# A hybrid trunk's first layer: convolution, time steps and head norms moved into the input projection

## The reference

```python
mods = silu(cvec) @ w_ada[l] + b_ada[l]            # shifts, scales, gates: sh1 sc1 g1 sh2 sc2 g2
h = rms(x, norm_w[l, 0]) * (1 + sc1) + sh1
u = h @ w_in                                       # 2832 columns: z, xbc, dt | q, k, v
xbc = silu(dwconv(xbc, conv_w, conv_b))            # 3 taps along the tokens, 768 channels -> xs, B, C
dt = softplus(dt_raw + dt_bias); g = dt * -exp(a_log)
y = bidirectional chunked scan(C, B, xs * dt, g)   # 8 heads of 64, both directions
y = rms((y + d_skip * xs) * silu(z), ssd_norm_w)
q, k = rms(q, q_norm), rms(k, k_norm)              # per head of 64
o = attention: context over context; each latent grid row over 8 rows + 128 cached keys
x = x + g1 * (concat(y, o) @ w_out)
h = rms(x, norm_w[l, 1]) * (1 + sc2) + sh2         # then the convolutional FFN
```

## Time and profile before

| | us |
|---|---|
| median of 3 runs | 3716.46 (3715.77 to 3718.22) |
| the profiled execution | 3712.03 |
| its span | 3710.4 |
| PE busy in the span | 3248.3 (88%) |
| DVE, ACT, POOL busy | 1863.4, 1364.7, 563.4 |
| mean granted TensorE clock | 0.936 of 2.4 GHz |

### The profile page before, as it was taken

How to read it: one execution, slowest core, us unless ns; L and a number is a source line. 1 busy time by engine, 2 the same in 40 slices (tenths; PEclk the granted TensorE clock), 3 DMA queues, 4 the chain that set the end, 5 groups by cost and what they waited for, 6 DMA issues and landing times. The chain is left out here.

```text
span 3710.4 us, 56967 instructions
## 1 busy us (share of the span) xinstructions
PE 3248.3 (88%) x22776; PEld 2966.8 (80%) x22776; DVE 1863.4 (50%) x3088; ACT 1364.7 (37%) x2312; POOL 563.4 (15%) x462
## 2 busy tenths in 40 slices
PE   5999386688939999999949999899978499999998
PEld 2999153466929999999929999677768499999998
DVE  4000366444277777753343300577753777777433
ACT  4111212676053333332233711455541433333322
POOL 1001064000033322200010001111100323221000
PEclk7999697899969999999979999899979699999999
DMA  6221501200021222164463521322122122222553
GB/s 279 84 92 46 215 4 72 104 2 24 23 92 67 82 72 72 49 214 145 131 244 109 167 90 47 138 89 86 66 101 75 36 72 84 77 72 71 201 170 130
DMA packets 133840, 370.12 MB, mean 100 GB/s; under 512 B 15232, under 2 KB 66816, under 8 KB 124496
## 3 DMA queue, kind: packets, MB, share of 16 engines
q1 hardware_dynamic: 124528, 335.82, 25.6%
q0 software_dynamic: 9056, 30.75, 2.3%
HBM read 282.56 MB, written 83.96 MB: 99 GB/s over the span
## 5 line engine op out<-in xcount | busy, mean ns | idle before, releaser
L83 PE MATMUL ffn__pair<-hf__acts,ffn__w_hi 128*128 128x288 f32 x2464 | 726.5, 295 | 115.0 <-DVE ffn__w_lo L807 115.0
L85 PE MATMUL ffn__pair<-hf__acts,ffn__w_hi 128*128 128x288 f32 x2464 | 728.5, 296 | 0.0
L84 PE MATMUL ffn__pair<-hf__acts,ffn__w_lo 128*128 128x288 f32 x2464 | 727.0, 295 | 0.0
L83 PEld LDWEIGHTS ffn__pair<-hf__acts,ffn__w_hi 128*128 128x128 f32 x2464 | 463.7, 188 | 116.3 <-DVE ffn__w_lo L807 116.3
L84 PEld LDWEIGHTS ffn__pair<-hf__acts,ffn__w_lo 128*128 128x128 f32 x2464 | 463.7, 188 | 0.0
L85 PEld LDWEIGHTS ffn__pair<-hf__acts,ffn__w_hi 128*128 128x128 f32 x2464 | 463.7, 188 | 0.0
L83 PE MATMUL ffn__pair<-hf__acts 128*128 128x384 f32 x1056 | 354.7, 336 | 8.5 <-DVE hf__acts L854 8.5
L85 PE MATMUL ffn__pair<-hf__acts 128*128 128x384 f32 x1056 | 354.4, 336 | 0.0
L84 PE MATMUL ffn__pair<-hf__acts 128*128 128x384 f32 x1056 | 354.4, 336 | 0.0
L83 PE MATMUL in__bank<-hm__h_lo,in__wt_hi 128*128 128x384 f32 x816 | 277.0, 340 | 10.3 <-DVE in__wt_lo L2053 5.3
L840 DVE SCALAR_TENSOR_TENSOR all__x_t<-all__x_t 128x127 f32<-128x127 f32 x352 | 271.2, 812 | 29.3 <-ACT all__x_t L709 29.2
(11 more groups left out here) (359 smaller groups left out, 6384.8 us busy)
## 6 DMA issues: line engine op xcount, KB each, us to landing
hf__raw<-w_down SPq DMA_DIRECT2D x100, 512.0 KB, 3.6
ffn_g<-all__x_t SPq DMA_DIRECT2D x44, 576.0 KB, 3.2
ffn__raw_odd<-ffn_g SPq DMA_DIRECT2D x132, 192.0 KB, 3.6
hf__raw<-w_up SPq DMA_DIRECT2D x44, 512.0 KB, 4.4
hm__raw<-w_t SPq DMA_DIRECT2D x34, 512.0 KB, 3.8
n0a__ada_w<-w_ada SPq DMA_DIRECT2D x16, 1024.0 KB, 10.3
n1a__ada_w<-w_ada SPq DMA_DIRECT2D x16, 1024.0 KB, 8.5
u_t<-in__out_t POOLq DMA_DIRECT2D x26, 576.0 KB, 3.1
```

The lines of the kernel that those rows point to most:

```text
L83: pe.matmul(out, w_hi, v_lo, start=first, stop=False)
L84: pe.matmul(out, w_lo, v_hi, start=False, stop=False)
L85: return pe.matmul(out, w_hi, v_hi, start=False, stop=last)
```

## The change

- The projection's tile order is now convolution, time steps, q, k; its loops are written out; the ring has four weight slots. While PE works on tile t, DVE, ACT and a few PE groups ("jobs", placed behind a bank of the next tile) process tile t-1: taps, SiLU and transposes; or squares, head sums, Ln, Exp and scaling. q and k go to `u0_t` already normed; convolution results stay in SBUF (`held`, and x_t's memory as `room`). The small chain of the time steps runs on DVE in the token half.
- Modulation groups 1 and 2 run in the token half of the projection, one step behind every second token block; the first norm keeps group 0, with 3 slots. Group 3 stays in the scan, with 2 slots in place of 4.
- The separate mask load, `conv_rows` and the head-norm block are gone, with their loads from device memory.
- Attention's keys, biases and values are loaded in the scan (`NaInputs.ahead`); q is loaded in the attention block, straight into `q_two`. Attention goes pair by pair.
- `y_tok` lies in x_t's memory; `out_project` loads x again from the input after the transposes.

```diff
-            ada = Modulation(s, d, mods, gains, ident, groups, 4, ps[NB:])
+            ada = Modulation(s, d, mods, gains, ident, groups, 3 if own_mods else 4, ps[NB:])
...
+def in_jobs():
+    jobs, after = [], {}
+    def put(t, b, job):
+        after.setdefault((t, b), []).append(len(jobs))
+        jobs.append(job)
+    for t in range(1, IN_TILES + 1):
+        prev = t - 1
+        if prev == DT_TILE:
+            put(t, 0, ("dt", 0, 0, 0))
+        elif prev < CONV - 1:
+            put(t, 1, ("conv", prev, 0, 4))
+            put(t, 1, ("conv", prev, 4, 4))
+            put(t, 2, ("conv", prev, 8, 1))
+        elif prev >= QK_FROM:
+            for b in range(NB):
+                put(t, b // 2, ("qk", prev - QK_FROM, b, 0))
+    return jobs, after
...
+                load(2)
+                load(3)
+                sp.dma_start(cw[:, :, :], d["ssd_conv"]).then_inc(small_in, 16)
+                sp.dma_start(half[:, :], d["half"]).then_inc(small_in, 16)
+                sp.dma_start(gain[:, :], d["qk_gain"]).then_inc(small_in, 16)
+                sp.dma_start(row[:, :], d["ssd_row"]).then_inc(row_in, 16)
+                sp.dma_start(tri[:, :, :], d["tri"]).then_inc(masks_in, 16)
+                ada.load_small(sp)
+                for n in range(ada.slots):
+                    ada.load(sp, n)
+                for t in range(4, IN_TILES):
+                    load(t)
...
+                ada.silu(act)
+                act.wait_ge(small_in, 48)
+                split_hi(0)
+                split_hi(1)
+                for t in range(IN_TILES):
                     for b in range(NB):
+                        evict(t, b)
+                        if b == 0 and 1 <= t <= CONV:
+                            silu(t - 1)
+                        for u in after.get((t, b), ()):
+                            read(u)
+                    split_hi(t + 2)
...
+                for t in range(IN_TILES):
+                    if t > QK_FROM:
+                        normalise(t - 1 - QK_FROM)
+                    if t < CONV:
+                        conv(t)
+                    elif t >= QK_FROM:
+                        square(t - QK_FROM)
+                    split_lo(t + 2)
+                normalise(IN_TILES - 1 - QK_FROM)
+                steps()
...
+                        if n % 2 and n // 2 < ada_steps:
+                            if n == 1:
+                                pe.wait_ge(t_out, NB * IN_TILES)
+                            if n // 2 == KT:
+                                ada.turn(pe, 0)
+                            ada.multiply(pe, n // 2)
...
-        ada = Modulation(s, d, mods, gains, ident, (3,), 4, ps[3:5])
+        ada = Modulation(s, d, mods, gains, ident, (3,), 2, ps[3:5])
...
-                sp.dma_start(dt[:, :, :, :].rearrange("p t w h -> p (t w h)"), d["u0_small"]).then_inc(dt_in, 16)
-                sp.dma_start(row[:, :], d["ssd_row"]).then_inc(row_in, 16)
                 sp.dma_start(state[:, 2:4, :], d["ssd_state"]).then_inc(state_in, 16)
                 sp.dma_start(z[:, :, :], d["u0_tok"][:, :, 0:SSD_W].rearrange("t p n -> p t n")).then_inc(z_in, 16)
                 ada.load_small(sp)
                 for n in range(ada.slots):
                     ada.load(sp, n)
+                for buffer, source, arrived in ahead:
+                    sp.dma_start(buffer, source).then_inc(arrived, 16)
...
-    units = [(r, p) for r in range(GRID_H) for p in range(PAIRS)] + [(None, h) for h in range(NA_H)]
+    units = [(r, p) for p in range(PAIRS) for r in range(GRID_H)] + [(None, h) for h in range(NA_H)]
...
+                for p in range(PAIRS):
+                    for e in range(2):
+                        rows = slice(64 * e, 64 * e + 64)
+                        sp.dma_start(q_two[rows, p, :, e, :],
+                                     d["u0_t"][p, rows, CTX:TOK].rearrange("p (r c) -> p r c", c=GRID_W))\
+                            .then_inc(q_in[p], 16)
...
+                    if r == 0:
+                        pe.wait_ge(q_in[p], 32)
+                        pe.wait_ge(blank, 2 * p + 2)
...
+                    if n == 1:
+                        for side in range(2):
+                            sp.wait_ge(turned, len(quads) // 2 * (side + 1))
+                            ks = slice(KT // 2 * side, KT // 2 * (side + 1))
+                            sp.dma_start(x_t[:, ks, :], x_from[:, ks, :]).then_inc(x_in[side], 16)
```

More of the change, by code:

```diff
@@ L94, with __init__ @@
 class Modulation:
-    def __init__(self, s, d, mods, gains, ident, groups, slots, ps):
+    def __init__(self, s, d, mods, gains, ident, groups, slots, ps, rows=None):
         self.d, self.mods, self.gains, self.ident, self.groups, self.slots = d, mods, gains, ident, groups, slots
@@ L913 @@
 TC = 256
[L916 to L920 removed]
+CONV = 6
+DT_TILE = CONV
+QK_FROM = CONV + 1
+IN_TILES = QK_FROM + 8
+RING = 4
+TOK_BANKS = (3, 4)
+def in_jobs():
[15 more added lines that the diff above has]
+    return jobs, after
@@ L921, in in_project @@
+def in_project(nc, tag, d, stored, h_hi, h_lo, room, held, ident, eps, raw, arrived, mods, gains):
+    n_tok = d["w0_tok"].shape[0]
+    jobs, after = in_jobs()
+    acc, sq = room[:, 0:2, :], room[:, 2:4, :]
+    x_tok = room[:, 4:8, :].rearrange("p k n -> p (k n)").rearrange("p (t n) -> p t n", n=SSD_W)
+    k_tok, k_t, q_t, dt, g, row, tri = (held[n] for n in ("k_tok", "k_t", "q_t", "dt", "g", "row", "tri"))
     with Scope(nc, tag) as s:
-        wt = load_split_ring(s, "wt", KT * P, raw=raw, arrived=arrived)
@@ new lines, in tok_raw, with weights, conv_out, last_job @@
+        def tok_raw(c):
+            return (raw, more)[c % 2][:, :, :].rearrange("p a n -> p (a n)")
+        def weights(t):
+            if t >= IN_TILES:
+                c = t - IN_TILES
+                return tok_raw(c), pair(c, w_hi), pair(c, w_lo)
+            return raw_of(t), w_hi[:, t % RING, :], w_lo[:, t % RING, :]
+        def conv_out(j):
+            return acc[:, j % 2, :] if j < 4 else (k_t, q_t)[j - 4][:, :]
+        def last_job(kind, j):
+            return max(u for u, job in enumerate(jobs) if job[0] == kind and job[1] == j) + 1
@@ L932, in in_project @@
+        n_parts = len([1 for job in jobs if job[0] == "conv"]) // (CONV - 1)
+        ada_steps = KT * len(ada.groups)
         with nc.Block() as block:
@@ L944, in _ @@
-                for c in range(2):
-                    load_tok(c)
-                with sp.Fori(1, loops) as i:
-                    for j in range(2):
-                        load_t(i, j)
-                load_t(loops, 0)
-                for c in range(2, n_tok):
-                    load_tok(c)
-            def split_hi(act, ring, slot, n, free=None):
-                act.wait_ge(ring["arrived"][slot], 16 * n)
-                if free:
-                    act.wait_ge(*free)
-                act.activation(ring["hi"][:, slot, :], ring["raw"][:, slot, :], ACT.Copy)\
-                    .then_inc(ring["hi_done"], 1)
@@ L966, in _ @@
+                for c in range(n_tok):
+                    load_tok(c)
+                for n in range(ada.slots, ada_steps):
+                    ada.load(sp, n)
+                sp.wait_ge(masks_in, 16)
             @block.scalar
             def _(act):
-                def evict_t(i, j, wait=True):
-                    if wait:
-                        act.wait_ge(t_stored[j], 16 * i)
-                    for b in range(NB):
-                        act.wait_ge(t_mm, NB * (2 * i + j) + b + 1)
-                        act.activation(out_t[:, j, b * BLK:(b + 1) * BLK], ps[3 * j + b][:, 0:BLK], ACT.Copy)\
-                            .then_inc(t_out, 1)
@@ new lines, in trunk @@
+                if l == 0:
+                    y_tok = x_t[:, :, :].rearrange("p k n -> p (k n)").rearrange("p (a t n) -> p a t n", a=2, t=NT)
+                    with Scope(nc, "nai") as ns:
+                        given = NaInputs(ns, d)
+                        ssd(nc, "ssd", d, y_tok, held, ident, ones, eps, mods, gains, given.ahead)
+                        na(nc, "na", d, y_tok, given, ident)
+                    out_project(nc, "out0", 0, d["w_out"][0], y_tok, ident, x_t, d["x_t"], mods)
```

667 lines of the change are left out of this document (290 added, 377 removed).

## The result

The changed kernel takes 3666.83 us, the median of 4 runs (3664.27 to 3669.29), against 3716.11 us of the kernel before in the same series (4 runs, 3710.88 to 3718.22): ratio 0.9868, interval 0.9856 to 0.988, 49.3 us less. The forecast was 3654, with a range of 3641 to 3676: the time lies inside, 13 us above the forecast. The profiled execution took 3664.27 us (span 3662.4), the one before 3712.0 (3710.4): 48.0 us less by the spans. A "step" is one `multiply` of four matmuls where the text speaks of the modulation, and one round of the chunked scan where it speaks of the scan; a "decay exponential" is ACT's large exponential of a scan step (`ssd__w`).

The account below looks back on a forecast made before the run. The prediction took PE to bound the projection's tile half, with two holes of little PE work around the scan. +2.2 +7.6 +35.1 -68.4 +2.0 +7.4 -0.7 -48.3 +1.0 = -62.1 us, from 3716.5 to 3654.4; range 3641 to 3676.

Parts of the forecast that it names:

- (a): Rival: attention's small-piece first load takes 20 to 30 us, or loads slow the scan; 3668 to 3680 us; chance 0.12.
- Step 3: Projection: added PE transposes, sums and modulation steps are paid in full, since PE has no idle time; +35.1 us.
- Step 4: Projection's end to scan's start: first decay exponential after 23.5 us, not 91.9, -68.4; second step at 1.2 GHz, +2.
- Step 5: Scan's end: two modulation weight slots, not four, delay the copy and the nine squares behind it; +7.4 us.
- Step 1: First norm: three weight slots, not four, make five chunks land behind PE's start; net +2.2 us.
- step 2: Projection's start: the SiLU, first in ACT's order, waits for small DMAs and holds the splits and PE; +7.6 us.
- Step 6: Attention's start: only pair 0 of q is waited for, taken as 7 us, bounds 4.0 and 9.5; -48.3 us.
- border: Between scan and attention: one scope with 37 semaphores in place of two with 44; -0.7 us.
- Step 7: Output projection: reloading x costs no wait, one more scope and 8 semaphores before it; +1.0 us.
- (b): Rival: the projection isn't PE-bound, one in-order wait costs 2 us a tile, 30 in all; 3684 us; chance 0.06.
- (d): Rival: the interleaved projection loses its clock; 63 us more at mean clock 0.84, the gain gone; chance 0.03.
- (c): Rival: covers are better than counted (SiLU's loads at 5.5, no clock loss, tail +4); 3641 to 3648 us; chance 0.12.

Follow-up runs that it names:

- left-out sums: Changed kernel with the 24 head-norm matmuls that sum squares left out of the projection; ratio 0.9826 to the kernel before.
- DVE's idle products: Changed kernel with 20 extra DVE products of 128x1152, results unused, put into the projection; ratio 0.9868 to the kernel before.
- mended order: Changed kernel with ACT's modulation-row copy behind the root and DVE's modulation add behind its nine products at the scan's end; ratio 0.9837 to the kernel before.
- undone loads: Changed kernel with the seven key, value and bias loads moved from the scan's queue to attention's, behind pair 0; ratio 0.9922 to the kernel before.
- repeated run: The changed kernel run once more, untouched, in the later series; 3664.77 us, ratio 0.9852 to the kernel before.
- kernel with pairs: Changed kernel with token-half modulation steps in pairs and the last head tile's store behind the first two token stores; 3662.38 us, ratio 0.984 to before.
- mended start: Changed kernel with the projection's first two weight splits ahead of the SiLU and PE's constants wait at tile 1; ratio 0.9831 to the kernel before.
- Three mended orders and one buffer: Changed kernel with splits before SiLU, copy behind root, SiLU at the scan's end and four first-norm weight slots; 3634.04 us, ratio 0.9774 to before.

## Why the prediction was right, and where it was off

The range held, but the narrower bounds of 3646 to 3666, which had 0.66 of the chances, were missed by 0.8 us, and no rival named that place: the result lies between them and (a). The order of the terms is as forecast: two holes closed for 119 us, 71 us of it given back at other places, 41 of them in the projection. The forecast's sum was -62.1, the spans give -48.0. Of the 14 us between them:

- **Step 3, +6.2.** This is the term that was mis-sized. The mechanism (PE has no idle time there, so each instruction is paid in full) is shown by the left-out sums and by DVE's idle products. By kind, from the distances of ACT's evictions: convolution 1.0 a tile, 5.0 (5.1 forecast); sums 24 x 0.67, 16.0 (15.4); row transposes 0.9 (0.9); steps 16 x 1.18, 18.9 (13.7); the wait behind the store 1.0 (0); the first tile -0.8, since PE reached full clock sooner (0). The step's price had been taken from its busy time without its surroundings. The bound for 57 insertions at 0.1 us, +6, nearly covered the whole (+6.2), but by luck: it is 16 of them at 0.32, and nearly nothing for the others. "No gap" also failed once, at the store.
- **Step 4, +2.1 and +2.7.** The border and the SiLU were right to 1.3 us. The second step came 4.1 later, not 2: I had the clock's 1.8, but not POOL, whose in-order queue holds the product for step 0 (which needs the small exponential) ahead of the mask for step 1. That term failed by half. The scan's later steps take 7.2 to 8.2 us (7.2 to 8.3 before) but for one that took 11.3 us at granted clock 0.50; that makes up the 2.7 there. It came some 70 us after the loads had landed (DMA share 0.00).
- **Step 5, +1.2.** Mechanism as forecast, shown by the mended order (-8.2). The steps' loads came a little later.
- **Step 1, +0.7 and step 2, +0.5.** The slot had also an effect on the chunk's load and on the clock.
- **Step 6, -1.3, and border, -0.1.** 5.8 us for the 7 taken between 4.0 and 9.5. The packets of the window take 31.7 ns each (67.3% of 16 engines for 28 us over 9520), while 8368 of the 9521 are under 512 B, at some 170 GB/s, where the large loads of the norm run at 420 (kernel before, 45 to 50 us). The Trainium skill (DMA: Bandwidth & Descriptors, Specifications) says that transfers under 512 B fall below line rate; this trace agrees, at 0.4 of the rate of the large ones. The prediction's estimate with it, 5.3 at half the rate, lies nearer to 5.8 than the 7 that I chose.
- **Step 7** was right on the waits: DVE's first update waits for PE. The +1.0 is right partly by luck: the border to the output projection grew by 0.5 us (1.6 to 2.1), and attention itself, put at 0, by 0.6 (203.9 to 204.5).
- **The unchanged rest, +3.4.** The forecast has it at nothing, since its code is the same. The whole runs of one kernel spread by 7 us and more, so this is not put down to the change.

Rivals: (a) falls with the 5.8 us for the small pieces and with the undone loads; (b) falls by DVE's idle products, and of its in-order waits one came, 1.0 us; (d) fell with the granted clock at 0.99 in the tile half and 1.00 in the token half; (c) did not come.

What stays open: the one long step of the scan. It stands at the same place in the repeated run and with the mended tail, at others in six more kernels, twice in the kernel with pairs, and in three kernels there is none: with the loads undone, with DVE's idle products, and with the mended start (its longest is 9.6 us at granted clock 0.82). Two of these three have the loads in the scan, so the loads don't suffice for it; no profile without them has it. The only profile of the kernel before doesn't have it, so whether the change brings it is not settled.

## What to carry to other kernels

When work of a serial stage moves into one that is bound by a single engine, its price there is the distance between that engine's neighbours with and without it, not its busy time; the short group of narrow matmuls here cost 0.32 us more at each visit, and two in a row paid that once, so put such groups together. What then decides is the head and the tail of each in-order queue: an instruction that is needed late but stands first (a SiLU for modulations, a copy ahead of nine squares, a store ahead of two others) held a whole stage here. Three mended orders and one buffer gave 30.7 us, where the whole change gave 52.7 in the same series. Before sizing a wait by the clock alone, look at which queue holds the next operand.

## What the runs showed of the hardware

- Going from 128-wide matmuls to a group of 4 with 32 columns and back costs 0.32 us in all beside the group's 0.86. Groups of 128x128 transposes (0.11 us each) and 384-wide sums (0.67 each, 0.64 forecast from their own length) between such matmuls show next to no addition. Why the one group has it and the others don't is not shown.
- TensorE's granted clock can fall in the midst of a stretch of steps that are all alike. A window of the changed kernel's scan, columns as above:

```profile
547.60:559.00 11.40, 11.40 (x40) 7.56 (x40) 5.75 (x11) 1.28 (x3) 4.82 (x4) 0.50 0.00 0
```

  PE's records fill this window since they last about twice as long (the four differences 3.78 us, 1.98 at full clock). In the 7.6 us before it PE was busy for 6.5 at granted clock 0.90, in the 7.0 after it for 6.0 at 0.95.
- The clock at one place differs from profile to profile of like code. In the first norm with four slots it stayed at 1.00 up to the copy in one profile (steps of 1.07 us) and fell to the 1.2 GHz level before it in three, the kernel before among them (1.93).
